# Second block of a two-block transformer: three groups of transposes two side steps later, and the compressed chain on VectorE in two pieces

## The chip, the cores and the metric

The kernel runs on one core of one Trainium2 chip. The metric is the device time of one execution in microseconds (us). Engines are named as in the profile: PE (TensorE), DVE (VectorE), ACT (ScalarE), POOL (GpSimd), SP (SyncE).

## What is computed

Two transformer blocks of two layers each, on 512 tokens of width 1024, in float32. The change is in the second block. One layer of it, cut to what matters:

```python
h = rmsnorm(x, norm_mix)
q_a, k_a, v_a, f_a, q_b, kv_b, g_b, gate_a, gate_b = split(h @ w_in)
o_a = fox_attention(...)                      # 8 heads with forget gates
y_a = from_heads(o_a) @ w_o_fox
q_n = partial_rope(to_heads(q_b, 8), pos)     # the turned queries
kc, vc, ks, vs, kw, vw = to_heads(kv_b)       # 2 key/value heads each
kc = partial_rope(compress_blocks(kc), ends)  # blocks of 32 tokens, stride 16
vc = compress_blocks(vc)                      # gelu(flat @ w1 + b1) @ w2 + b2
o_c = softmax(q_n kc) vc                      # 31 compressed blocks
o_s, o_w = selected and window branches       # over ks, vs and kw, vw
o_n = g0 * o_c + g1 * o_s + g2 * o_w
mixed = sigmoid(gate_a) * y_a + sigmoid(gate_b) * (o_n @ w_o_nsa)
x = x + mixed @ w_out
h = rmsnorm(x, norm_mlp); x = x + relu(h @ w_up)**2 @ w_down
```

With 512 tokens the selected and the window branch both see all causal keys, so both are plain causal attention.

## The kernel before, in words

Weights stream from HBM in units of up to 512 KB. SP loads a unit into RAW, ACT copies it to its upper float32r part Wh (L1466), DVE subtracts to get the lower part Wl (L2192), and PE makes three products per tile from the upper and lower parts (`three`, L641 to L643). The copies and subtractions run two units ahead of PE (`AHEAD`).

Each of PE, ACT and DVE has a program of its own, written out in order. Beside the main stream of linear layers each program keeps a list of side generators (`Sides`); `tick()` advances every open one to its next `yield`. The main stream calls `tick()` at the same places in the three programs, so one `yield` is one side step on all of them, and `idle(n)` lets n steps pass. The text numbers the steps T0, T1, ... from the first tick of the first `hidden` unit. In most units there are six products of 512 columns between two ticks; in the units of `hidden` (the compressor's first layer) three products of 256 columns. The stream from T0 is: four `hidden` units of keys, alternating with two `ga` units, then an `oa` unit, the same for values, then `ga`, `oa`, `ga`, `oa` and 32 steps of `gb` (T80 to T111), four ticks in each unit. Then `drain(ont)` ends the sides, and the `ob` products with ONh and ONl follow. Order within an engine is fixed: a waiting instruction holds all behind it.

The sides that matter, with PE's lines:

- `nsa_side` (L1246 ff.): after `idle(5)` six transposes of turned queries and keys (`heads_side`, L975 through `turn_rows`), `idle(5)`, then `mixing` over 64 items. An item is a query tile of 128 rows, a branch and a head. In step i, item i has its scores (L964, L965, mask L960), item i - 3 its exponentials transposed (L901), and a finished pair of items is multiplied with the values (L922, L923). Between scores and transposes lie the maximum on DVE (L2500), the exponential on ACT (L1663), the reciprocal on DVE (L2505, emitted one step after the maximum, behind the next item's maximum) and the normalising on POOL (L3291). Items come as tiles 3, 3, 0, 0 (4, 4, 1, 1 blocks of 128 keys) in the first 32 and 2, 2, 1, 1 in the last 32.
- `keys_side` (L1285 ff.): transposes of the compressor's inner layer HT (L1290), its second layer (L1299, L1300) and for keys a further transpose (L1307); once for keys (`kv` 0), begun after the first four `hidden` units, and once for values.
- `compressed_side` (L1314 ff.): for the later and then the earlier half of the tokens, scores on compressed keys (L1324, L1325), a pause, the transposes of their normalised exponentials CB (L1337); on DVE mask, maximum and shift (L3096 to L3102), sum, reciprocal, gates (L3106 to L3113), the multiplication (L3119); on ACT the exponential (L2056). At its end it adds `("compressed", l)` to `done`. `mixing` may not close a sum of the last 32 items before that (`need`).
- `on_side` splits the finished sums ONS into ONh (ACT) and ONl (DVE) once `mixing` and `compressed_side` are done.

Of the kernel before, what the change touches and what calls it, by code (L numbers as in the profile page):

```python
# [476 lines left out]
def idle(n):  # L477

    for _ in range(n):
        yield  # L480
# [22 lines left out]
def over(ap, n, where):  # L503
    v = ap.unsqueeze(where)
    shape = list(v.shape)
    shape[where] = n
    return v.to_broadcast(shape)
# [109 lines left out]
def tensor_program(pe, M, G, K, plan):  # L617
# [577 lines left out]
    for l in range(DEPTH):  # L1195
# [50 lines left out]
        def nsa_side():  # L1246
# [5 lines left out]
            while ("keys", l) not in done:  # L1252
                yield
            yield from idle(5)
            for j in range(6):
# [29 lines left out]
        def keys_side(kv):  # L1285
            yield from idle(2)
            b = fresh(f"ht{l} {kv}")
# [27 lines left out]
        def compressed_side():  # L1315
            for c in (1, 0):
# [12 lines left out]
                K.close(f"cs{l} {c}")  # L1329
                yield  # L1330
                yield
                yield
                yield
                b = fresh(f"ct{l} {c}")
# [111 lines left out]
def scalar_program(sc, M, G, K, plan, a):  # L1446
# [462 lines left out]
    for l in range(DEPTH):  # L1909
# [100 lines left out]
        def nsa_side():  # L2010
            while fox in sides.open:
                yield
            yield from blocks_side()
            done.add(("blocks", l))
            while ("keys", l) not in done:
                yield
            yield from idle(5)
            for j in range(6):
                yield from heads_side(j)
            yield from idle(5)  # L2020
            yield from mixing(nsa_bundles(l), take=nsa_take, need=("compressed", l), tail=5)
# [14 lines left out]
        def keys_side(kv):  # L2036
            yield from idle(3)
            name = f"ht{l} {kv}"
# [12 lines left out]
        def compressed_side():  # L2051
            for c in (1, 0):
# [3 lines left out]
                sc.activation(M.CB[:, :], M.CB[:, :], ACT.Exp).then_inc(G.c_exp, 1)  # L2056
                yield
                yield
                yield
                if c == 1:  # L2060
# [111 lines left out]
def vector_program(ve, M, G, K, plan):  # L2172
# [699 lines left out]
    for l in range(DEPTH):  # L2872
# [147 lines left out]
        def nsa_side():  # L3020
# [12 lines left out]
            for j in range(2):  # L3033
# [9 lines left out]
                yield  # L3043
            yield from idle(2)
            for j in range(6):
# [11 lines left out]
        def keys_side(kv):  # L3057
            yield from idle(7)
            name = f"w2{l} {kv}"
# [23 lines left out]
        def compressed_side():  # L3083
# [4 lines left out]
            for c in (1, 0):  # L3088
# [25 lines left out]
                if c == 0:  # L3114
                    p0 = p4[:, 0, :, :]
                    i = ve.tensor_tensor(p0, p0, over(M.CST[:, C_XV:C_XV + 32], 8, 1), ALU.mult)
                i.then_inc(*own.up())
                ve.wait_ge(*own.now())
                ve.tensor_tensor(p3, p3, over(f2.rearrange("p a b -> p (a b)"), 32, 2), ALU.mult).then_inc(G.c_p, 1)  # L3119
                yield  # L3120
                yield
# [240 lines left out]
```

## Time and profile before

| | us |
|---|---|
| median of 3 runs | 2856.04 |
| lowest and highest run | 2851.41, 2857.71 |
| the profiled execution | 2851.48 |
| its span in the trace | 2849.7 |
| PE busy, share of the span | 2730.9, 96% |
| DVE busy | 1556.9, 55% |
| ACT busy | 1157.8, 41% |
| POOL busy | 132.1, 5% |

The span is what the trace covers; 1.8 us lie around it. Matmuls are pipelined, so the busy time of PE counts overlaps as busy; where PE really stands still is seen in the time line, which puts the idle time before an instruction and its releaser in brackets. The changed part of each of the second block's two layers lies at about 1362 to 1588 and 2189 to 2415 us.

### The profile page before, as it was taken

The numbers are of one execution on the slowest core, as the hardware profiler recorded it, in microseconds if no ns is written. First come the engines' busy times: TensorE is split into PE (matmuls) and PEld (weight loads), VectorE is DVE, ScalarE is ACT, GpSimd is POOL, SyncE is SP. The second block draws the span as 40 slices with busy tenths as digits, with TensorE's granted clock in tenths as the row PEclk, the third lists the DMA queues.
The fourth block names the chain that finished last, engine by engine and source line by source line (L and its number), as shares of the span: only waits on it lengthen the run. The fifth ranks groups of instructions, "written<-read, shape, count | busy, mean of one in ns | idle before, by whom it ended". The sixth has DMA issues, their size and how long they took to land.

```text
span 2849.7 us, 34790 instructions
## 1 busy us (share of the span) xinstructions
PE 2730.9 (96%) x13497; PEld 2249.6 (79%) x13497; DVE 1556.9 (55%) x2788; ACT 1157.8 (41%) x2078; POOL 132.1 (5%) x221
## 2 busy tenths in 40 slices
PE   7899999999999999989899999999989899999997
PEld 6778888887788888767778888888768778888886
DVE  7856444467564444576766653343667665643343
ACT  3554222235542222355654433242465644342331
POOL 1000000000000000011122000000010211000000
PEclk9999999998999999999999999999999999999999
DMA  4102232321022323321311233333212211323332
GB/s 121 52 23 86 96 97 98 99 87 56 22 87 96 96 96 97 92 67 54 103 45 45 90 95 96 97 98 99 88 45 89 68 45 60 104 90 98 99 99 75
DMA packets 186358, 231.40 MB, mean 81 GB/s; under 512 B 11874, under 2 KB 140356, under 8 KB 186196
## 3 DMA queue, kind: packets, MB, share of 16 engines
q1 hardware_dynamic: 184500, 225.95, 25.4%
q0 software_dynamic: 976, 1.32, 0.3%
q8 instruction: 108, 1.77, 0.3%
q10 hardware_dynamic: 720, 1.92, 0.2%
q14 instruction: 54, 0.44, 0.1%
HBM read 227.05 MB, written 2.11 MB: 80 GB/s over the span
## 4 chain that ended last, share of the span: by engine, by line
PE 79%; DVE 12%; ACT 5%; issue 3%; DMA 0%; POOL 0%; ACTq 0%; DVEq 0%
PE bank L641 23%; PE bank L643 23%; PE bank L642 23%; DVE Wl L2192 2%; ACT Wh L1466 1%; PE bank L901 1%; PE bank L846 1%; DVE STT L2500 1%; PE bank L922 1%; PE bank L923 1%; PE bank L964 1%; PE bank L831 1%; PE bank L1155 1%; PE bank L965 1%; DVE KAl L2240 1%
## 5 line engine op out<-in xcount | busy, mean ns | idle before, releaser
L2192 DVE TENSOR_TENSOR Wl<-RAW,Wh 128x1024 fp32r<-128x1024 f32 (+3 forms) x434 | 510.5, 1199 | 367.1 <-ACT Wh L1466 366.2
L1466 ACT ACTIVATE Wh<-RAW 128x1024 fp32r<-128x1024 f32 (+3 forms) x434 | 437.7, 1032 | 402.7 <-PE bank L643 402.2
L641 PE MATMUL bank<-Hh,Wh 128*128 128x512 f32 (+1 forms) x1104 | 450.4, 408 | 6.3 <-DVE Wl L2192 4.9
L643 PE MATMUL bank<-Hh,Wl 128*128 128x512 f32 (+1 forms) x1104 | 433.3, 393 | 0.0
L642 PE MATMUL bank<-Hl,Wh 128*128 128x512 f32 (+1 forms) x1104 | 433.1, 392 | 0.0
L641 PE MATMUL bank<-HA,Wh 128*128 128x512 f32 x704 | 274.2, 390 | 0.0
L642 PE MATMUL bank<-HA,Wh 128*128 128x512 f32 x704 | 273.9, 389 | 0.0
L643 PE MATMUL bank<-HA,Wl 128*128 128x512 f32 x704 | 273.9, 389 | 0.0
L641 PEld LDWEIGHTS bank<-Hh,Wh 128*128 128x128 f32 (+1 forms) x1104 | 208.1, 188 | 48.9 <-DVE Wl L2192 6.2
L643 PEld LDWEIGHTS bank<-Hh,Wl 128*128 128x128 f32 (+1 forms) x1104 | 207.2, 188 | 46.9
L642 PEld LDWEIGHTS bank<-Hl,Wh 128*128 128x128 f32 (+1 forms) x1104 | 208.2, 189 | 36.3
L641 PE MATMUL bank<-A,Wh 128*128 128x512 f32 x608 | 236.5, 389 | 0.0
L642 PE MATMUL bank<-A,Wh 128*128 128x512 f32 x608 | 236.5, 389 | 0.0
L643 PE MATMUL bank<-A,Wl 128*128 128x512 f32 x608 | 236.5, 389 | 0.0
L1663 ACT ACTIVATE P<-bank,STT 128x384 f32<-128x384 f32 (+1 forms) x192 | 101.3, 528 | 137.8 <-DVE STT L2500 136.7
L643 PEld LDWEIGHTS bank<-HA,Wl 128*128 128x128 f32 x704 | 132.1, 188 | 27.6
L642 PEld LDWEIGHTS bank<-HA,Wh 128*128 128x128 f32 x704 | 132.1, 188 | 27.4
L641 PE MATMUL bank<-Wh,Hh 128*128 128x512 f32 (+2 forms) x384 | 149.2, 389 | 4.7 <-DVE Wl L2192 4.7
L641 PEld LDWEIGHTS bank<-HA,Wh 128*128 128x128 f32 x704 | 132.2, 188 | 27.1
L643 PE MATMUL bank<-Wh,Hl 128*128 128x512 f32 (+2 forms) x384 | 144.1, 375 | 0.0
L642 PE MATMUL bank<-Wl,Hh 128*128 128x512 f32 (+2 forms) x384 | 144.0, 375 | 0.0
L2324 DVE TENSOR_TENSOR XT<-bank,XT 128x512 f32<-128x512 f32 x112 | 77.1, 690 | 121.0 <-PE bank L643 120.8
(394 smaller groups left out, 4690.2 us busy)
## 6 DMA issues: line engine op xcount, KB each, us to landing
RAW<-in_w_up_dram SPq DMA_DIRECT2D x108, 512.0 KB, 3.6
RAW<-in_w_down_dram SPq DMA_DIRECT2D x108, 512.0 KB, 3.7
RAW<-in_w_in_dram SPq DMA_DIRECT2D x90, 512.0 KB, 3.5
RAW<-in_w_gate_dram SPq DMA_DIRECT2D x44, 512.0 KB, 3.6
RAW<-in_w_out_dram SPq DMA_DIRECT2D x28, 512.0 KB, 3.7
RAW<-in_cmp_w_dram SPq DMA_DIRECT2D x16, 512.0 KB, 3.8
RAW<-in_w_o_fox_dram SPq DMA_DIRECT2D x8, 512.0 KB, 3.4
RAW<-in_w_o_nsa_dram SPq DMA_DIRECT2D x8, 512.0 KB, 3.4
```

Source lines behind the costliest of these rows:

```text
L641: pe.matmul(o, sh, mh, start=first, stop=False)
L642: pe.matmul(o, sh, ml, start=False, stop=False)
L643: return pe.matmul(o, sl, mh, start=False, stop=last)
L831: x = pe.transpose(b[:, k * P:(k + 1) * P], M.PB[:, i % 4, k * P:(k + 1) * P], ident)
L846: x = pe.matmul(b[:, h * 64:(h + 1) * 64], M.PT[:, i % 3, k * P:(k + 1) * P], values(g, h, kb[k]), start=k == 0, stop=k == len(kb) - 1)
L901: x = pe.transpose(b[:, k * P:(k + 1) * P], e[:, k * P:(k + 1) * P], ident)
L922: pe.matmul(b[:, c:c + w], v, ph, start=B.opens(n) and k == 0, stop=False, skip_group_check=True)
L923: x = pe.matmul(b[0:64, c:c + w], v[:, 0:64], pl, start=False, stop=k == len(kb) - 1, skip_group_check=True)
L1466: sc.activation(M.Wh[:, v % NHL, 0:n], M.RAW[:, v % NRAW, 0:n], ACT.Copy).then_inc(G.w_hi, 1)
L1663: sc.activation(e, M.bank[K.of(name)][:, 0:e.shape[1]], ACT.Exp, bias=M.STT[:, 0, t, h:h + 1], accum_out=M.STT[:, 1, t, h:h + 1]).then_inc ...
L2192: ve.tensor_tensor(M.Wl[:, v % NRAW, 0:n], M.RAW[:, v % NRAW, 0:n], M.Wh[:, v % NHL, 0:n].bitcast(F32), ALU.subtract).then_inc(G.w_lo, 1)
L2324: ve.tensor_tensor(M.XT[:, k, :], M.bank[K.of(name)][:, :], M.XT[:, k, :], ALU.add).then_inc(*K.empties(name))
```

## The change

Nothing is computed otherwise; side steps are moved. Two more steps pass on all three engines before the transposes of turned queries and keys (with them all of `mixing`), before the transposes of HT, and between the compressed scores and the transposes of CB. On DVE the multiplication that ends the compressed chain (L3119) gets a step of its own, one after the sum, the reciprocal and the gates.

```diff
 # PE and ACT, nsa_side
-            yield from idle(5)
+            yield from idle(7)
             for j in range(6):
                 yield from heads_side(j)
 # PE, keys_side (ACT: 3 to 5, DVE: 7 to 9)
-            yield from idle(2)
+            yield from idle(4)
             b = fresh(f"ht{l} {kv}")
 # PE, compressed_side
                 K.close(f"cs{l} {c}")
-                yield
-                yield
-                yield
-                yield
+                yield from idle(6)
                 b = fresh(f"ct{l} {c}")
 # ACT, compressed_side
                 sc.activation(M.CB[:, :], M.CB[:, :], ACT.Exp).then_inc(G.c_exp, 1)
-                yield
-                yield
-                yield
+                yield from idle(5)
 # DVE, nsa_side
-            yield from idle(2)
+            yield from idle(4)
             for j in range(6):
                 yield from heads_side(j)
 # DVE, compressed_side
                 i.then_inc(*own.up())
+                yield
                 ve.wait_ge(*own.now())
                 ve.tensor_tensor(p3, p3, over(f2.rearrange("p a b -> p (a b)"), 32, 2), ALU.mult).then_inc(G.c_p, 1)
+                yield
                 yield
                 yield
```

By step numbers, PE has the first query transposes at T7 instead of T5, the first HT at T32 instead of T30, item i of `mixing` at T34 + i instead of T32 + i, the first transposes of CB at T75 instead of T71 and the second at T85 instead of T79. The compressed part is complete at T88 instead of T82. Item 45, the first of the last 32 to close a sum, is due at T82 before and at T84 now, so `mixing` is held one step before and five now, and ends at T107 instead of T101. The order of loads on SP and of the normalising on POOL is the same.

DVE, the compressed chain of the later half, before (CB are the compressed exponentials, CF the gates over their sums, STT the running maxima and sums of `mixing`):

```order
L2500 TENSOR_REDUCE STT_69<-bank 128x1 [waits bank5_full]
L2505 RECIPROCAL STT_69<-STT_69 128x1 [waits bank2_drained]
L2240 TENSOR_TENSOR PT_59<-bank,PT_58 128x2x128 [waits part_hi_made]
L3106 TENSOR_REDUCE RS_70<-CB_154 128x16 [waits cmp_exp_made]
L3110 RECIPROCAL CF_152<-RS_70 128x16 [waits vector_own]
L3113 TENSOR_TENSOR CF_152<-CF_152,GS_151 128x16 [waits bank1_drained,vector_own]
L3119 TENSOR_TENSOR CB_154<-CB_154,CF_152 128x512 [waits vector_own]
L2500 TENSOR_REDUCE STT_69<-bank 128x1 [waits bank7_full]
```

The same place in the changed kernel:

```order
L2500 RECIPROCAL STT_69<-STT_69 128x1 [waits bank6_drained]
L2235 TENSOR_TENSOR PT_59<-bank,PT_58 128x2x128 [waits part_hi_made]
L3101 TENSOR_REDUCE RS_70<-CB_154 128x16 [waits cmp_exp_made]
L3105 RECIPROCAL CF_152<-RS_70 128x16 [waits vector_own]
L3108 TENSOR_TENSOR CF_152<-CF_152,GS_151 128x16 [waits bank1_drained,vector_own]
L2357 TENSOR_TENSOR M_88_136<-bank,RBB_163 128x512 [waits bank1_drained,bank1_full]
L2495 TENSOR_REDUCE STT_69<-bank 128x1 [waits bank3_full]
L2500 RECIPROCAL STT_69<-STT_69 128x1 [waits bank2_drained]
L2235 TENSOR_TENSOR PT_59<-bank,PT_58 128x3x128 [waits part_hi_made]
L3115 TENSOR_TENSOR CB_154<-CB_154,CF_152 128x512 [waits vector_own]
L2495 TENSOR_REDUCE STT_69<-bank 128x1 [waits bank0_full]
```

A gate's evacuation (M) and one item's maximum, reciprocal and split now stand between the gates and the multiplication.

PE at T38, the third of the four short steps of the first `hidden` unit of values, before (XHL are the compressor's inputs, P the exponentials, KSh and KSl the keys, QN the queries):

```order
L641 MATMUL bank<-Wh_54,XHL_129 64x256
L642 MATMUL bank<-Wl_53,XHL_129 64x256
L643 MATMUL bank<-Wh_54,XHL_130 64x256
L901 MATMUL bank<-CST_61,P_9_57 128x128 [waits score_exp_normed,bank3_drained]
L964 MATMUL bank<-KSh_133,QN_132 128x128 [waits bank4_drained]
L965 MATMUL bank<-KSl_134,QN_132 128x128
L960 MATMUL bank<-CMB_65,IDB_64 128x128
L922 MATMUL bank<-PT_58,VN_125 128x256 [waits bank4_drained,bank7_drained,bank2_drained]
```

The same step in the changed kernel:

```order
L641 MATMUL bank<-Wh_54,XHL_129 64x256
L642 MATMUL bank<-Wl_53,XHL_129 64x256
L643 MATMUL bank<-Wh_54,XHL_130 64x256
L901 MATMUL bank<-CST_61,P_9_57 128x128 [waits score_exp_normed,bank2_drained]
L901 MATMUL bank<-CST_61,P_9_57 128x128 x3
L964 MATMUL bank<-KSh_133,QN_132 128x512 [waits bank3_drained]
L965 MATMUL bank<-KSl_134,QN_132 128x512
L960 MATMUL bank<-CMB_65,IDB_64 128x128
```

Before, this step transposes item 3 (one block) and makes the scores of item 6; now it transposes item 1 (four blocks) and makes the scores of item 4.

ACT where `mixing` is held for the compressed part, before (ONS are the sums, M the gates, PT the transposed exponentials):

```order
L1663 ACTIVATE P_9_57,STT_69<-bank,STT_69 128x256 [waits bank0_full,score_max_made]
L1984 ACTIVATE ONS_135<-bank 64x2x128 [waits bank3_full,bank6_full]
L1984 ACTIVATE ONS_135<-bank 64x2x128
L1466 ACTIVATE Wh_54<-RAW_52 128x1024 [waits bank3_full,raw_in1]
L1512 ACTIVATE PT_58<-bank 128x3x128 [waits bank3_full,bank6_full]
L1663 ACTIVATE P_9_57,STT_69<-bank,STT_69 128x256 [waits bank5_full,score_max_made]
L2098 ACTIVATE M_89_137<-M_89_137 128x512 [waits bank1_drained]
```

And in the changed kernel:

```order
L1660 ACTIVATE P_9_57,STT_69<-bank,STT_69 128x384 [waits bank0_full,score_max_made]
L1463 ACTIVATE Wh_54<-RAW_52 128x1024 [waits bank0_full,raw_in1]
L2093 ACTIVATE M_89_137<-M_89_137 128x512 [waits bank3_drained]
L2093 ACTIVATE M_89_137<-M_89_137 128x512 [waits bank6_drained]
L1463 ACTIVATE Wh_54<-RAW_52 128x1024 [waits weights_used,raw_in2]
L1509 ACTIVATE PT_58<-bank 128x2x128 [waits bank3_full,values_mixed]
L1660 ACTIVATE P_9_57,STT_69<-bank,STT_69 128x256 [waits bank7_full,score_max_made]
L1981 ACTIVATE ONS_135<-bank 64x2x128 [waits bank3_full,bank5_full]
```

A whole weight unit and both of its gates now pass without an exponential of `mixing` between them.

## Rows read from the trace of the kernel before

**Rows 1.** The page, part 4: the chain that ended last, by engine

```profile
PE 79%; DVE 12%; ACT 5%; issue 3%; DMA 0%; POOL 0%; ACTq 0%; DVEq 0%
```

**Rows 2.** Time line of PE, first pass: start us, us, instruction [idle before <-releaser]

```profile
1362.85 0.66 PE L975 MATMUL bank<-CST,QNS 128*128 128x128 f32 x4 [1.35 <-DVE QNS L2389]
...
1385.96 0.30 PE L1290 MATMUL bank<-CST,HT 64*128 64x64 f32 x2 [1.30 <-ACT HT L2033]
...
1389.38 0.47 PE L964 MATMUL bank<-KSh,QN 128*128 128x512 f32 x1 [1.11 <-issue]
...
1401.37 0.30 PE L901 MATMUL bank<-CST,P 128*128 128x128 f32 x1 [1.95 <-POOL P L3291]
...
1419.21 0.30 PE L901 MATMUL bank<-CST,P 128*128 128x128 f32 x1 [1.99 <-POOL P L3291]
...
1437.60 0.30 PE L901 MATMUL bank<-CST,P 128*128 128x128 f32 x1 [1.63 <-POOL P L3291]
...
1441.13 0.63 PE L901 MATMUL bank<-CST,P 128*128 128x128 f32 x4 [1.65 <-POOL P L3291]
...
1486.10 0.52 PE L901 MATMUL bank<-CST,P 128*128 128x128 f32 x3 [0.37 <-POOL P L3291]
...
1489.04 1.09 PE L1337 MATMUL bank<-CST,CB 128*128 128x128 f32 x4 [2.11 <-DVE CB L3119]
...
1515.45 0.63 PE L1337 MATMUL bank<-CST,CB 128*128 128x128 f32 x4 [1.66 <-DVE CB L3119]
```

**Rows 3.** Waits of PE, 2185 to 2410 (second pass): us in total, times, longest

```profile
PE bank L1337 <- DVE CB L3119: 3.8, 2, 2.1
```

**Rows 4.** Time line of PE, first pass: first products of a short and of long steps

```profile
1357.23 0.28 PE L641 MATMUL bank<-Wh,XHL 128*64 128x256 f32 x1
...
1358.59 0.40 PE L641 MATMUL bank<-Hh,Wh 128*128 128x512 f32 x1
...
1361.11 0.39 PE L643 MATMUL bank<-Hh,Wl 128*128 128x512 f32 x1
```

**Rows 5.** Time line of DVE, 1387 to 1403

```profile
1387.88 1.40 DVE L2552 TENSOR_TENSOR KSl<-bank,KSh 64x512 fp32r<-64x512 f32 x2
...
1398.80 1.21 DVE L2192 TENSOR_TENSOR Wl<-RAW,Wh 128x1024 fp32r<-128x1024 f32 x1
1399.93 0.67 DVE L2500 TENSOR_REDUCE STT<-bank 128x1 f32<-128x512 f32 x1
...
1402.05 0.27 DVE L2500 TENSOR_REDUCE STT<-bank 128x1 f32<-128x128 f32 x1
```

**Rows 6.** Time line of ACT, 1387 to 1403

```profile
1397.09 0.37 ACT L1663 ACTIVATE P<-bank,STT 128x128 f32<-128x128 f32 x1
...
1397.45 1.05 ACT L1466 ACTIVATE Wh<-RAW 128x1024 fp32r<-128x1024 f32 x1
...
1400.64 0.69 ACT L1663 ACTIVATE P<-bank,STT 128x512 f32<-128x512 f32 x1 [1.66 <-DVE STT L2500]
```

**Rows 7.** Time line of POOL, 1387 to 1403

```profile
1400.78 0.45 POOL L3291 TENSOR_SCALAR P<-P,STT,GS 128x128 f32<-128x128 f32 x1 [3.10 <-DVE STT L2505]
1402.03 0.78 POOL L3291 TENSOR_SCALAR P<-P,STT,GS 128x512 f32<-128x512 f32 x1 [0.81 <-DVE STT L2505]
```

**Rows 8.** Windows: us, busy time of each engine, granted share of PE's clock, DMA

```profile
1420.26:1423.67 3.41, 3.41 (x17) 3.31 (x16) 1.09 (x5) 1.68 (x8) 1.33 (x3) 0.50 0.25 68
1488.50:1491.94 3.44, 2.90 (x9) 2.55 (x10) 2.39 (x5) 1.51 (x3) 0.56 (x1) 0.50 0.05 16
2318.00:2321.40 3.40, 3.40 (x12) 2.72 (x11) 1.49 (x2) 1.28 (x3) 0.47 (x1) 0.50 0.00 0
```

**Rows 9.** Time line of PE, 1573 to 1589

```profile
1574.05 0.28 PE L923 MATMUL bank<-PT,VN 128*64 128x256 f32 x1
...
1587.81 0.39 PE L641 MATMUL bank<-ONh,Wh 128*128 128x512 f32 x1
```

**Rows 10.** Time line of DVE, 1573 to 1589

```profile
1579.29 1.29 DVE L2240 TENSOR_TENSOR ONl<-ONS,ONh 128x512 fp32r<-128x512 f32 x2 [1.22 <-ACT ONh L2090]
```

More of the change, by code:

```diff
@@ L2016, in nsa_side @@
                 yield
-            yield from idle(5)
+            yield from idle(7)
             for j in range(6):
@@ L2036, in keys_side @@
         def keys_side(kv):
-            yield from idle(3)
+            yield from idle(5)
             name = f"ht{l} {kv}"
@@ L2056, in compressed_side @@
                 sc.activation(M.CB[:, :], M.CB[:, :], ACT.Exp).then_inc(G.c_exp, 1)
-                yield
-                yield
-                yield
+                yield from idle(5)
                 if c == 1:
@@ L3057, in keys_side @@
         def keys_side(kv):
-            yield from idle(7)
+            yield from idle(9)
             name = f"w2{l} {kv}"
```

## The prediction

> **What bounds the kernel now.** I read four views in this order. The chain of waits says which engine sets the end: PE holds 79% of it, DVE and ACT the rest in small pieces [rows 1], so a wait counts only where PE itself stands idle. The time line of PE in the first pass of the changed part (layer 0 of the second block, about 1362 to 1588 us) then names each of its idle pieces in brackets [rows 2]: turned queries not ready (1.35 us), the compressor's inner layer HT not ready (1.30), the first score of the selected branch waiting without a named releaser (1.11), waits for POOL's normalised exponentials (1.95, 1.99, 1.63, 1.65, and a fifth of 0.37), and the two transposes of the compressed exponentials CB (2.11, 1.66). The waits of the second pass repeat this: the two CB waits there also add up to 3.8 [rows 3], so I work out one pass and double it. Third, what one side step covers: between two steps stand either three products of 256 columns or six of 512. Twelve of the first kind take 1358.59 - 1357.23 = 1.36 us, 0.34 a step; of the second kind eleven starts take 1361.11 - 1358.59 = 2.52 us, 0.229 each, 1.37 a step [rows 4]. Last, the granted clock by stretch [rows 8].
>
> **The change part by part.** No instruction is added or removed; all of them move, on PE, ACT and DVE alike, and with them POOL's normalising, which follows the items. The weight loads' queue issues in the same order as before. Number the steps T0, T1, ... from the first `hidden` unit. PE has short steps of 0.34 us at T0 to 3, 8 to 11, 16 to 19, 24 to 31, 36 to 39, 44 to 47, 52 to 55, long ones of 1.37 elsewhere up to T111.
>
> - *Turned queries, T5 to T7.* Two long steps, 2.7 us of products, now stand ahead, against a wait of 1.35 [rows 2]: gain 1.35.
> - *Inner layer's transpose, T30 to T32.* The hidden products it needs end at T27 as before, but the K transposes move as well, and ACT's copies of them stand ahead of the copy to HT. Between the last K transpose and this one, a short step becomes a long one: cover grows by 1.37 - 0.34 = 1.03, so of 1.30 some 0.3 stay. PE, no longer held before, then comes early to a weight unit whose Wl stands in DVE's queue behind the moved query and key parts; between nothing and the 1.30 itself I put 0.5. Gain 0.5 (ends 0 and 1.3).
> - *First score, T32 to T34.* It waits for the last key part KSl, whose DVE pair ends at 1387.88 + 1.40 = 1389.28 [rows 5], 0.1 ahead of it. From the last K transpose to the first score two short steps become long: cover +2.06, of which the shrunk waits ahead take 1.0. Of 1.11 about 0.2 stay. Gain 0.9 (ends 0 and 1.11).
> - *Compressed chain.* The transposes of CB come six steps after the last compressed score instead of four; the multiplication by the gates gets a step of its own, still with two PE steps behind it where there was one. The multiplication gains one long step with its item's products, over 1.37; what stood right ahead of it on DVE (sum, reciprocal, gates) gains two, over 2.74, against 2.11 and 1.66 [rows 2]. Both waits go: gain 3.77 (low end 2 x 1.37 = 2.74, if the multiplication alone was late).
>
> Gains: 1.35 + 0.5 + 0.9 + 3.77 = 6.52 us a pass.
>
> What is late next? The mixing starts two steps later, so the short steps now meet other items. Items come in fours: two of 4 blocks, two of 1 (for the first half). At T36, T44 and T52 a unit begins, and the next Wh and Wl are made there. Before, the item ahead of that border had one block: its exponential (0.37) is followed on ACT by Wh (1.05), then on DVE by Wl (1.21), the next item's maximum (0.67) and only then its reciprocal, and POOL (0.45) [rows 5 to 7]. That is the wait of 1.95. Now it is a 4-block item: exponential 0.69 and POOL 0.78 instead of 0.37 and 0.45, +0.65; the maximum in between is of one block, 0.27 for 0.67 [rows 5], -0.40; and PE's own work in the three steps is some 0.15 less. So the wait stays at the same step and grows by 0.4, three times: loss 1.2. The first item now has its turn inside the short steps too: loss 0.4, a fifth of a border wait. In the last stretch a second item waited already (1.65 [rows 2]); with two large items at once I add 0.4. Ends for all of this: a gain of 1.65 (that second wait goes) and a loss of 5 (a second wait of 1.65 in each stretch).
>
> Around T73 the score chain loses cover: the shift by the maximum, two DVE passes over CB, now stands a step ahead of a border, so that exponential, Wh, Wl and reciprocal follow it in one line. The wait at this place is 0.37 now, at 1486.10 [rows 2]. I let it grow by 0.7, between 0 and the 1.6 that would make it a border wait of 1.99.
>
> Last, the tail. The compressed part is complete at T88 instead of T82, and the mixing may not close its second half before that: it is held five steps instead of one. So it ends six steps later, four steps ahead of the products with ONh instead of ten. From the last value product (1574.05 + 0.28) to those products there are 13.5 us now [rows 9], and there will be 4 x 1.37 = 5.5. The last ONl is ready 1580.58 - 1574.33 = 6.25 us after it [rows 9, 10], and is asked for by the fourth group of three products, 3 x 0.69 = 2.1 after the start, at 7.5. It fits by about 1.3; I put 0.4 (ends 0 and 3.8, below).
>
> Losses: 1.2 + 0.4 + 0.4 + 0.7 + 0.4 = 3.1. Net gain 6.52 - 3.1 = 3.4 a pass, **6.8 us** in both.
>
> **The clock.** Behind the wait of 1.99 and behind that of 2.11 PE ran at 0.50 of full speed, 1.2 GHz, for 3.41 us each; the stretch from 2318.00 in the second pass is one more [rows 8]. Each costs about half its length, 1.7. Two of the three stand behind CB waits that go: a credit of 3.4. But three border waits a pass grow beyond 2 us, and one of those of 1.99 drew such a stretch already; I let one more a pass do so: 0 in sum, ends -3.4 and +3.4. The Trainium skill (TensorE: Matmul & The Clock Gate, section "Why this matters for your kernels") lets the speed fall only behind idle gaps longer than any in these rows; by it the clock would give and take nothing, and the sum would be the waits alone, 6.8 again. The rows differ from it: the granted 0.50 stands right behind 1.99 and 2.11.
>
> The profiled execution took 2851.48 us; the sum makes 2844.7 of it. It is the low end of the three runs (2851.41 to 2857.71); from their median, 2856.04, the same 6.8 gives **2849.2**, which I predict. A measurement of this kernel can tell about 0.2%, 5.7 us, from no change.
>
> **The rivals.**
> - *The short steps take all of it back.* If both large items wait in each of the three stretches, as the pair of 1.63 and 1.65 does, the loss there is about 5 instead of 2: net 6.52 - 6.1 = 0.4 a pass, 2855. For it: that pair; against: the first two stretches show one wait each.
> - *Slower: the tail.* If the evacuations of the last gates stand ahead of the taking of the last sums on ACT and DVE, two on each engine (0.7 apiece, as 512-column pieces take [rows 5, 6]) and one Wh and Wl (1.05, 1.21), 5.0 us in all, the chain is 11.3 against 7.5: PE waits 3.8 and a half-speed stretch behind it costs 1.7. That is 5.5 instead of 0.4: net 6.52 - 8.2 = 1.7 slower a pass, 2859. It decides once the tail costs PE more than 0.4 + 3.4 = 3.8 a pass. Against it: the same chain took 6.25 with evacuations around it.
> - *Clean.* The border waits stay as they are, the tail costs nothing and the clock's credit comes in full: (6.52 - 0.7) x 2 + 3.4 = 15, 2841. For it: the smaller maximum that now stands in the border chain; against: the larger exponential there.
>
> **How the numbers follow.** The forecast (net 3 to 10 us faster) gets 0.62, of which about two thirds are beyond 5.7 us; the first rival 0.19; the slower one 0.09, most of it beyond the bound once a noisy median is added; the clean one 0.10. So faster 0.41 + 0.10 = 0.51, the same 0.21 + 0.19 + 0.01 = 0.41, slower 0.08. The range runs from the clean case, 2841, to between the first rival and the slower one, 2857, and leaves out about 2 in 10.
>
> **What would show it.** In the changed profile: no PE wait for QNS and none for CB; HT and first score under 0.5; one POOL wait of about 2.3 at each of the three borders, at a product with four transposes instead of one; a new POOL wait near 1 us between the two transposes of CB; 24 products between the last value product and the first with ONh, with under 0.5 of waiting there. Wrong: a CB wait over 0.5; border waits in pairs; over 2 us of waiting at the first products with ONh; a half-speed stretch behind more than two of a pass's three borders.

## The result, and the profile after

The changed kernel takes 2840.26 us (median of four runs, 2838.24 to 2840.70) against 2855.0 for the kernel before (four runs): a ratio of 0.9948, 95% interval 0.9936 to 0.996, or 14.7 us faster (11 to 18). The forecast was 6.8 us. The direction was right, the size less than half; the time lies 0.7 us below the range and at the rival "clean".

| us | before | after |
|---|---|---|
| median | 2855.0 | 2840.26 |
| profiled execution | 2851.48 | 2838.24 |
| its span | 2849.7 | 2836.4 |
| PE busy | 2730.9 | 2727.1 |
| DVE busy | 1556.9 | 1555.4 |
| POOL busy | 132.1 | 132.4 |

The chain of waits of the changed kernel has three points less of PE than [rows 1]; DVE and ACT still come in small pieces. So again a wait counts where PE stands.

```profile
PE 76%; DVE 14%; ACT 5%; issue 4%; DMA 0%; POOL 0%; ACTq 0%; DVEq 0%
```

The time line of PE shows where. First the kernel before: a value product of the first attention in either layer, whose wait of 1.43 the change does not touch (the mark of the pass), the first product with ONh in the second pass (that of the first pass is in [rows 9]), and, at 1467.94, a wait for PT in the first pass that [rows 2] leave out.

```profile
1295.04 0.38 PE L922 MATMUL bank<-PT,VF 128*128 128x256 f32 x1 [1.43 <-DVE PT L2240]
...
1467.94 0.44 PE L964 MATMUL bank<-KSh,QN 128*128 128x384 f32 x1 [0.69 <-DVE PT L2240]
...
2121.79 0.38 PE L922 MATMUL bank<-PT,VF 128*128 128x256 f32 x1 [1.43 <-DVE PT L2240]
...
2416.56 0.39 PE L641 MATMUL bank<-ONh,Wh 128*128 128x512 f32 x1
```

The same marks after, and between the first two of them every wait of PE in the changed part of the first pass (start, length, the instruction; idle time before it and its releaser in brackets; behind the edits, line numbers are three to five lower than before, so L3288 here is L3291 there):

```profile
1295.22 0.38 PE L922 MATMUL bank<-PT,VF 128*128 128x256 f32 x1 [1.43 <-DVE PT L2235]
...
1383.99 0.50 PE L641 MATMUL bank<-Hh,Wh 128*128 128x512 f32 x1 [0.43 <-DVE Wl L2187]
...
1389.56 0.47 PE L964 MATMUL bank<-KSh,QN 128*128 128x512 f32 x1 [0.53 <-issue]
...
1395.01 0.63 PE L901 MATMUL bank<-CST,P 128*128 128x128 f32 x4 [0.96 <-POOL P L3288]
...
1397.54 1.09 PE L901 MATMUL bank<-CST,P 128*128 128x128 f32 x4 [1.31 <-POOL P L3288]
...
1416.19 0.63 PE L901 MATMUL bank<-CST,P 128*128 128x128 f32 x4 [2.07 <-POOL P L3288]
...
1434.85 0.63 PE L901 MATMUL bank<-CST,P 128*128 128x128 f32 x4 [1.95 <-POOL P L3288]
...
1437.02 0.30 PE L901 MATMUL bank<-CST,P 128*128 128x128 f32 x1 [0.36 <-POOL P L3288]
...
1439.92 0.38 PE L922 MATMUL bank<-PT,VN 128*128 128x256 f32 x1 [0.27 <-DVE ONS L2994]
...
1445.16 0.63 PE L901 MATMUL bank<-CST,P 128*128 128x128 f32 x4 [0.52 <-POOL P L3288]
...
1489.31 0.52 PE L901 MATMUL bank<-CST,P 128*128 128x128 f32 x3 [1.10 <-POOL P L3288]
...
1493.80 0.47 PE L641 MATMUL bank<-OAh,Wh 128*128 128x512 f32 x1 [0.36 <-DVE PT L2235]
...
1581.94 0.39 PE L641 MATMUL bank<-ONh,Wh 128*128 128x512 f32 x1
...
1583.67 0.50 PE L641 MATMUL bank<-ONh,Wh 128*128 128x512 f32 x1 [0.20 <-DVE ONl L2235]
...
2116.90 0.38 PE L922 MATMUL bank<-PT,VF 128*128 128x256 f32 x1 [1.43 <-DVE PT L2235]
...
2402.30 0.39 PE L641 MATMUL bank<-ONh,Wh 128*128 128x512 f32 x1
```

By the marks the 13.3 us by which the span is shorter split exactly. Up to the first mark 0.18 is lost. The first pass, mark to ONh, shrinks from 1587.81 - 1295.04 = 292.77 to 286.72: 6.05 gained. From there to the second mark 0.98 is lost (533.98 to 534.96). The second pass shrinks from 294.77 to 285.40: 9.37. From its ONh to the end 0.96 is lost (433.14 to 434.10). 6.05 + 9.37 - 0.18 - 0.98 - 0.96 = 13.30.

Neither QNS nor CB has a wait any more; the brackets of the changed part of the first pass, 15.1 in [rows 2] and 0.69 for PT, 15.8 together, are down to 10.1. The two passes differ by the clock. Windows of the kernel before (us, busy time of each engine, granted share of PE's clock, DMA), beside the stretches of [rows 8]:

```profile
1395.00:1430.00 35.00, 31.06 (x192) 25.45 (x191) 22.60 (x62) 20.12 (x53) 9.46 (x16) 0.95 0.20 61
1484.00:1496.00 12.00, 9.52 (x51) 7.64 (x50) 8.17 (x20) 5.63 (x15) 2.45 (x4) 0.86 0.15 44
2225.00:2240.00 15.00, 13.02 (x75) 10.70 (x74) 10.34 (x30) 8.67 (x25) 3.98 (x7) 0.89 0.18 58
2290.00:2325.00 35.00, 31.72 (x179) 25.93 (x177) 22.30 (x57) 15.80 (x41) 5.79 (x10) 0.90 0.16 46
2297.49:2300.90 3.41, 3.41 (x12) 2.73 (x11) 0.25 (x1) 0.47 (x3) 0.32 (x1) 0.50 0.00 0
```

and of the changed kernel, where in the changed part nothing but these two is below 1.00:

```profile
1390.00:1425.00 35.00, 30.65 (x184) 24.79 (x183) 22.93 (x59) 19.11 (x51) 8.79 (x14) 0.90 0.20 61
2210.00:2245.00 35.00, 30.11 (x185) 23.74 (x183) 24.14 (x61) 20.63 (x53) 8.32 (x14) 0.95 0.20 61
```

A share of 0.95 in 35 us is 1.7 us of the fast clock lost, one stretch of 3.4 us at 1.2 GHz. Before there are two stretches in the first pass and three in the second, 8.6 us lost; now two and one, 5.2. (The 35 us from 2290 hold two: that of [rows 8] and the one in the last window, behind a wait of 0.69 for PT, which [rows 8] leave out as they do the one after 2225.) So of the second pass's 9.37 about 6.0 are waits, as in the first pass, where the number of stretches stays, and 3.4 are clock.

### The profile page after: what moved, and what is told of

Its sections match the earlier page's. It is cut to its first block, busy times and chain, and to the rows that moved or that the text cites. A ratio compares the mean times of both kernels' runs of the same rounds, so it can differ in the third digit from the quotient of the medians.

```text
span 2836.4 us, 34790 instructions
## 1 busy us (share of the span) xinstructions
PE 2727.1 (96%) x13497; PEld 2244.0 (79%) x13497; DVE 1555.4 (55%) x2788; ACT 1157.3 (41%) x2078; POOL 132.4 (5%) x221
## 3 DMA queue, kind: packets, MB, share of 16 engines
HBM read 227.05 MB, written 2.11 MB: 81 GB/s over the span
## 4 chain that ended last, share of the span: by engine, by line
PE 76%; DVE 14%; ACT 5%; issue 4%; DMA 0%; POOL 0%; ACTq 0%; DVEq 0%
PE bank L641 22%; PE bank L642 22%; PE bank L643 22%; DVE Wl L2187 2%; ACT Wh L1463 2%; PE bank L901 1%; PE bank L846 1%; DVE STT L2495 1%; PE bank L922 1%; PE bank L964 1%; PE bank L1155 1%; PE bank L965 1%; PE bank L831 1%; PE bank L923 1%; DVE KAl L2235 1%
```

## The experiments

The kernels ran in three sets of four, each set beside runs of the kernel before (medians 2855.81, 2855.48 and 2856.19). Diffs are against the kernel before unless said otherwise and show PE's program; ACT and DVE get the same number of steps at their places.

**1. The compressed chain's part alone.**

```diff
                 K.close(f"cs{l} {c}")
-                yield
...
+                yield from idle(6)
```

(`...` stands for three more `yield`. On DVE the multiplication gets a step of its own, as in the change.)

> The compressed chain's part alone (six steps between its scores and its transposes, the multiplication in a step of its own); the mixing and the inner layer stay where they were. If the parts simply add up by the forecast's terms: both CB waits go (3.77 us a pass), 0.7 comes back around T73 and 0.4 at the tail: 5.3 us faster in both passes. If they add up by what the changed kernel's rows show (1.10 - 0.37 and 0.36 around T73, 0.96 at the tail): 1.95 a pass, 3.9 faster, and up to 3.4 more where the half-speed stretches behind the CB waits go with them. If the parts need each other (the mixing's moved items were part of the cure): a CB wait over 0.5 us stays, and the gain is under 2 us.

Measured: 2845.66 (seven runs), ratio 0.9968 (0.9957 to 0.9979), 10.2 us faster. The two CB waits in the first pass of its PE time line:

```profile
1497.32 0.66 PE L1334 MATMUL bank<-CST,CB 128*128 128x128 f32 x4 [0.69 <-DVE PT L2235]
...
1523.58 0.63 PE L1334 MATMUL bank<-CST,CB 128*128 128x128 f32 x4 [0.27 <-DVE CB L3115]
```

They fall from 2.11 and 1.66 to 0.69 (now put down to PT) and 0.27, the other waits stay: 2.8 us a pass. No stretch at 0.50 stands behind the first any more. The tail costs nothing: 433.16 from ONh to the end, as before. From mark to ONh its passes take 289.99 and 290.37, 7.2 us less than before in both, which fits 5.6 of waits and one half-speed stretch less. The medians say 10.2; what the rest is, this profile does not show. By the medians this part is two thirds of the gain.

**2. Turned queries and mixing two steps later, alone.**

```diff
-            yield from idle(5)
+            yield from idle(7)
             for j in range(6):
                 yield from heads_side(j)
```

> The turned queries and with them the mixing two steps later, nothing else. By the forecast's terms: QNS 1.35 and the first score 0.9 go, the borders cost 1.2 + 0.4 + 0.4: 0.25 a pass, 0.5 us faster in both. By the changed kernel's rows: QNS 1.35, first score 0.58 and the PT wait 0.69 go, the borders cost 0.22: 2.4 a pass, 4.8 faster. If the parts need each other: the copies of the moved K transposes now stand on ACT ahead of the copy to HT, whose transposes have not moved, so the HT wait grows from 1.30 towards 3, the CB waits do not shrink, and the kernel is 0 to 4 us slower.

Measured: 2857.19 (eleven runs), 1.0005 (0.9996 to 1.0014). QNS is gone, and two waits grow in its place:

```profile
1385.78 0.31 PE L1290 MATMUL bank<-CST,HT 64*128 64x64 f32 x2 [2.57 <-ACT HT L2033]
...
1488.25 1.09 PE L1337 MATMUL bank<-CST,CB 128*128 128x128 f32 x4 [3.98 <-DVE CB L3119]
```

HT waits 2.57 instead of 1.30, and the first CB 3.98 instead of 2.11. The third theory held. The forecast had seen the first of the two ("ACT's copies of them stand ahead of the copy to HT"), not the second: the moved items also make the compressed chain later.

**3. The inner layer's transposes two steps later, alone.**

```diff
         def keys_side(kv):
-            yield from idle(2)
+            yield from idle(4)
```

> The transposes of the inner layer HT two steps later, nothing else. By the forecast's terms: of HT's 1.30 some 0.3 to 0.5 stay and Wl may come late by as much: 1 to 2 us faster in both passes. By the changed kernel's rows (HT gone, Wl 0.43 new): 0.87 a pass, 1.7 faster. If the parts need each other: HT's wait goes, but the first score right behind it waits longer by the same amount (1.11 to about 2), since PE comes to it earlier: 0 to 1 us faster.

Measured: 2856.80 (eleven runs), 1.0005 (0.9996 to 1.0014). HT's wait of 1.30 goes and comes back at the next unit, as 1.64 for Wl:

```profile
1388.28 0.50 PE L641 MATMUL bank<-Hh,Wh 128*128 128x512 f32 x1 [1.64 <-DVE Wl L2192]
```

The second CB waits 2.35 for 1.66, while the waits for PT and POOL ahead of the first CB shrink by as much (0.69 to 0.32, 0.37 to none). None of the theories had Wl at 1.64; the gain is nil, as the third said.

**4. The whole change, with the multiplication in the step of the gates.**

```diff
                 i.then_inc(*own.up())
-                yield
                 ve.wait_ge(*own.now())
                 ve.tensor_tensor(p3, p3, over(...), ALU.mult).then_inc(G.c_p, 1)
+                yield
                 yield
```

(DVE, against the changed kernel.)

> The whole change but for the split: on DVE the multiplication follows the gates in the same step, as before, with two more steps behind it. If the split matters (the multiplication in the way of the next item's maximum, reciprocal and POOL): the POOL wait near T74, 1.10 in the changed kernel, grows by the multiplication's time and the kernel is 1 to 3 us slower than the changed one. If the later transposes alone do the work: the CB waits are gone as well, all PE waits within 0.3 us of the changed kernel's, the time within 2 us of it (about 0.995 of the kernel before).

Measured: 2842.04 (five runs), 0.9952 (0.9938 to 0.9966). The POOL wait is the changed kernel's 1.10, and no CB wait stands in either pass:

```profile
1494.91 0.52 PE L901 MATMUL bank<-CST,P 128*128 128x128 f32 x3 [1.09 <-POOL P L3288]
```

The split buys nothing that shows; the two later steps do the work.

**5. Mixing and inner layer later, the compressed chain as before.**

> Turned queries, mixing and inner layer two steps later, the compressed chain as before: the change without its third part. If the three parts simply add up (compressed chain alone 10 us faster, mixing alone 1 slower, inner layer alone 1 slower): about 2 us slower than the kernel before. If mixing and inner layer only help each other (HT wait 2.57 and Wl wait 1.64 of the two alone fall to the changed kernel's 0.43) and the compressed chain is a matter of its own: QNS, HT and PT waits go, CB waits stay at 2.1 and 1.7, 2 us a pass, about 4 us faster. If the moved mixing makes the compressed chain late as well (CB waits 4.0 and 1.5 as with the mixing alone): 1.7 of those 2 us are given back and it is 0 to 1 us faster.

The diffs of 2 and 3 together. Measured: 2852.91 (eleven runs), 0.9993 (0.9985 to 1.0002): 2.6 us faster, if anything. HT's wait is gone and Wl's is 0.43, so these two parts help each other. But:

```profile
1493.63 0.63 PE L1337 MATMUL bank<-CST,CB 128*128 128x128 f32 x4 [3.93 <-DVE CB L3119]
...
1521.04 0.63 PE L1337 MATMUL bank<-CST,CB 128*128 128x128 f32 x4 [2.66 <-DVE CB L3119]
```

6.6 us of CB waits a pass instead of 3.8. So the parts do not add up in waits: the compressed part alone takes 2.8 us a pass from the brackets, but 4.9 once the mixing is moved (15.0 here, 10.1 in the changed kernel). A step at this place is also worth more than its 1.37 us of products, as the items' own products lie in it: from the last compressed score of the later half PE has 11.65 us here until it stands still for CB (1478.05 to 1489.70), and 17.70 in the changed kernel until the transposes of CB (1475.11 to 1492.81), of which 1.10 is the new wait for POOL. So two steps hold 4.95 us of work, not 2.74.

**6. The kernel before, with PE kept at work in the CB waits.**

```diff
                 b = fresh(f"ct{l} {c}")
+                for k in range(16 if c else 12):
+                    pe.transpose(b[:, k % 4 * P:k % 4 * P + P], ident, ident)
                 pe.wait_ge(G.c_p, 2 * l + 2 - c)
```

> The kernel before, with PE kept at work in the two CB waits: 16 and 12 extra transposes of the identity into the bank that the real transposes then overwrite, some 1.4 and 1.1 us of the waits of 2.11 and 1.66. If PE's clock falls because PE stands idle there: the half-speed stretches behind the CB waits (at 1488 and 2316 in the kernel before) are gone, the waits' ends stay, and the kernel is 1.7 to 3.4 us faster by its clock alone. If these stretches have nothing to do with the idle time: they remain, and the time is that of the kernel before within 1 us.

The extra transposes are overwritten by the real ones. Measured: 2851.65 (eleven runs), 0.9989 (0.998 to 0.9997), 3.8 us faster by the medians. Of the wait before the first CB 0.28 is left. Windows from there on, and around the second pass's:

```profile
1488.00:1500.00 12.00, 11.37 (x79) 9.59 (x77) 9.09 (x23) 6.68 (x17) 3.01 (x5) 1.00 0.15 45
2290.00:2325.00 35.00, 33.57 (x206) 27.80 (x205) 23.24 (x58) 16.13 (x42) 5.76 (x10) 0.95 0.16 46
```

The first window is at 1.00 where the kernel before had 0.86, the second at 0.95 where it had 0.90: the two stretches behind the CB waits are gone, the third (behind the PT wait at 2296) is not. PE's real work did not start earlier. Behind the waits that were not filled, stretches come and go from one profile to the next: the first pass has two at its borders where the kernel before has one, and is no shorter (292.87 us from mark to ONh, 292.77 before); the second has none at its borders and takes 291.64 instead of 294.77. So the time is better taken from the medians, and their 3.8 us (1 to 6 by the interval) fit the 3.4 of two stretches. The clock's credit is real.

**7. Mixing five steps later, the compressed chain as in the change.**

```diff
-            yield from idle(5)
+            yield from idle(10)
             for j in range(6):
                 yield from heads_side(j)
```

(And the diff of 1.)

> Turned queries and mixing five steps later, the compressed chain as in the change, the inner layer where it was before. With five (as with one) step the two items that stand at a border of units are both of one block: exponential 0.37, maximum 0.28 and POOL 0.45 beside Wh and Wl, and the first border passes before there are exponentials to transpose. If the borders are set by the items' size there: the wait at the first border goes (2.3 in the changed kernel), the other two fall to about 1.5 each or less, the first score's and PT's waits go; HT's stays near 1.5; 3 to 5 us a pass better than the changed kernel, 2830 to 2834. If a border costs about 2 us whatever stands there (the four measured border waits were 1.95 to 2.07): the same time as the changed kernel, within 3 us, or slower by a tail that now ends three steps later (up to 4 us a pass).

Measured: 2816.99 (four runs), 0.9864 (0.9851 to 0.9877): 38.5 us faster than the kernel before, 23 better than the change. These are all its waits of the first pass from QNS on, but for one of 0.25:

```profile
1387.70 0.31 PE L1290 MATMUL bank<-CST,HT 64*128 64x64 f32 x2 [1.16 <-ACT HT L2030]
...
1400.66 0.63 PE L901 MATMUL bank<-CST,P 128*128 128x128 f32 x4 [1.16 <-POOL P L3288]
...
1412.56 0.30 PE L901 MATMUL bank<-CST,P 128*128 128x128 f32 x1 [0.71 <-POOL P L3288]
...
1428.21 0.30 PE L901 MATMUL bank<-CST,P 128*128 128x128 f32 x1 [0.23 <-POOL P L3288]
```

```profile
1360.00:1575.00 215.00, 211.26 (x1274) 174.95 (x1273) 150.11 (x343) 126.48 (x291) 38.93 (x64) 1.00 0.23 69
```

The border waits are 0.71 and 0.23, and in neither pass does the clock fall (this window is the first pass's, from QNS on). The passes last 275.53 and 275.18 from mark to ONh. It is more than either theory gave: the borders were put at 1.5 and have 0.71 and 0.23, the last stretch, T73 and the tail have no wait left, and the changed kernel's three stretches at 1.2 GHz are gone.

**8. Mixing five steps later and nothing else.**

> As the run before, but with the compressed chain as in the kernel before: turned queries and mixing five steps later and nothing else. If the CB waits come from the mixing's work ahead of the chain on DVE, ACT and POOL at this place: they change with the items there, to under 1 us each, and the kernel is within 5 us of the run before. If the compressed chain is late by its own length: CB waits of 2.1 and 1.7 or more stay, and it is 7 to 10 us slower than the run before.

Measured: 2820.28 (four runs), 0.9877 (0.9862 to 0.9892). One number is changed, 5 to 10 on PE and ACT and 2 to 7 on DVE. The second CB waits no longer, the first half as long as before:

```profile
1496.32 0.63 PE L1337 MATMUL bank<-CST,CB 128*128 128x128 f32 x4 [1.05 <-DVE CB L3119]
```

So the CB waits depend mostly on which items stand beside the chain (3.98 for the first with two steps in run 2, 1.05 with five), not on its length alone; a wait just over the 1 us of the first theory is left.

**9 and 10. Mixing one step later, and four steps later.** The compressed chain is as in the change; the first `idle` is 6, then 9.

> Turned queries and mixing one step later instead of two, the compressed chain as in the change, the inner layer as before. The items at a border are then both of one block, as with five steps, but the first border is met. If the border waits are set by which items stand there: waits of about 0.7 at the first two borders and 0.2 at the third (as with five steps: 0.71 and 0.23), the first score's wait stays partly, and the time is 2820 to 2826, 14 us or more under the changed kernel though the mixing starts earlier. If it was only the later start that helped with five steps: the borders keep about 2 us each and the time lies between those of the compressed part alone (2846) and of the change (2840).

> Turned queries and mixing four steps later, the rest as in the run before: the same items at the borders as in the kernel before (one block, then four), but the first border is passed before there are exponentials to transpose. If the border waits are set by which items stand there: 1.99 at the second border, 1.63 and 1.65 at the third as in the kernel before, the first gone: 4.3 us a pass slower than with five steps, 2825 to 2832 with the clock. If the later start is what matters: within 3 us of the run with five steps, 2815 to 2820.

Measured: 2826.59 (0.9899, 0.9884 to 0.9914) with one step, 2837.31 (0.9938, 0.9922 to 0.9955) with four, four runs each. The waits at the first two borders with one step:

```profile
1399.74 0.30 PE L901 MATMUL bank<-CST,P 128*128 128x128 f32 x1 [1.05 <-POOL P L3288]
...
1416.26 0.30 PE L901 MATMUL bank<-CST,P 128*128 128x128 f32 x1 [0.72 <-POOL P L3288]
```

and with four:

```profile
1397.40 1.09 PE L901 MATMUL bank<-CST,P 128*128 128x128 f32 x4 [2.94 <-POOL P L3288]
...
1415.92 0.30 PE L901 MATMUL bank<-CST,P 128*128 128x128 f32 x1 [1.98 <-POOL P L3288]
```

Later is not better: with one step 1.05, 0.72 and 1.21, with four 2.94, 1.98 and 1.42. With four the second border has the kernel before's 1.99 again, as its items are the same ones. Both expectations missed at one end, and the time with four steps lies above both of its ranges: with one step the third border does not fall to 0.2 (1.21, and another 0.59 follows there; why, stays open) and HT waits 2.27; with four the first border is not passed, since the first transposes come in the last step of its short stretch. The kernels with none, one, two, four and five steps agree with this: what decides is which items of the group of four stand at a border. With one step and with five they are the two small ones, with large ones ahead whose products PE works off meanwhile (this last is argued, not tested by itself).

**11. Five steps later, with the inner layer's two steps as in the change.**

> As the run with five steps, but with the inner layer two steps later as in the change. If the wait for HT (1.16 with five steps) simply goes: 2.3 us faster, about 2815. If it only moves on to what comes behind it (as with the inner layer alone, where HT's wait became one for Wl of 1.64): the same time or slower, 2817 to 2825, with new waits at the second layer or at the compressed chain.

The diffs of 7 and 3. Measured: 2830.39 (four runs), 0.9912 (0.9897 to 0.9926): 13 us slower than without this part, more than any theory gave. HT's 1.16 is gone and comes back several times over: there is 0.60 ahead of the second layer's products (L1299), POOL's 1.16 and 0.71 are 1.84 and 1.06, there is one of 1.09 for PT between the two CBs, and at the first CB

```profile
1485.50 0.63 PE L1334 MATMUL bank<-CST,CB 128*128 128x128 f32 x4 [1.19 <-DVE CB L3115]
```

and the tail's wait for ONl, 0.20, which run 7 did not have. Each pass also has a stretch at 1.2 GHz again (from 1400.14 and from 2308.08). Here the part of the change that it needs at two steps does harm.

**12. The changed kernel, with PE kept at work in the border waits.**

```diff
             b = fresh(f"{tag} t{i}")
+            if need:
+                for k in range({1: 8, 9: 16, 17: 16}.get(i, 0)):
+                    pe.transpose(b[:, k % 4 * P:k % 4 * P + P], ident, ident)
             pe.wait_ge(*norm.due())
```

> The changed kernel, with PE kept at work in the border waits: 8, 16 and 16 extra transposes of the identity into the bank that the real ones then overwrite, some 0.7, 1.4 and 1.4 us of waits of 1.3, 2.1 and 1.95. If PE's clock falls because it stands idle at the borders: the half-speed stretches there (at 1396 and 1416 in the first pass, 2220 in the second of the changed kernel) are gone, and the time is 3 to 5 us under the changed kernel's, 2835 to 2837. If not: stretches as before, 2840.

Measured: 2837.14 (four runs), 0.9936 (0.9921 to 0.9951). Around the borders, where the changed kernel had 0.90 and 0.95:

```profile
1390.00:1430.00 40.00, 37.81 (x241) 30.77 (x241) 28.89 (x70) 25.14 (x61) 9.69 (x16) 1.00 0.22 64
2210.00:2245.00 35.00, 32.84 (x216) 26.78 (x216) 25.33 (x64) 21.92 (x55) 8.79 (x14) 1.00 0.22 63
```

The passes last 283.80 and 283.83 from mark to ONh, 2.9 and 1.6 less than the changed kernel's, for two and one stretches. The medians, 3.1 apart, agree, but the intervals of the two ratios overlap, so the time alone does not show it. The windows do: nothing in either pass is below 1.00, while run 4, with the same border waits not filled, has 0.90 and 0.95 around them as the changed kernel has, and run 5 has 0.95 and 0.95.

## Why the prediction was wrong

Term by term, us of a pass, from the brackets of [rows 2] and of the time line above:

| term | forecast | measured |
|---|---|---|
| QNS | +1.35 | +1.35 |
| HT, less the new wait for Wl | +0.5 | 1.30 - 0.43 = +0.87 |
| first score | +0.9 | 1.11 - 0.53 = +0.58 |
| CB | +3.77 | +3.77 |
| PT wait at 1467.94 | not counted | +0.69 |
| three borders, first item, last stretch | -2.0 | -0.22 |
| around T73 | -0.7 | 0.37 - 1.10 - 0.36 = -1.09 |
| tail | -0.4 | -0.97 |
| net | +3.4 | 6.05 - 0.97 = +5.1 |

The measured terms above the tail sum to 5.95, and the marks give 6.05. The PT wait is one of PE's idle pieces that [rows 2] leave out, so the prediction could not count it. Both passes: 10.2 instead of 6.8. The clock: 3.4 instead of 0. Together 13.5, and the profiled executions are 13.3 apart.

**The step that failed** is the one on the short steps: "the wait stays at the same step and grows by 0.4, three times", with 0.4 more for the first item and 0.4 for the last stretch. Forecast as a loss of 2.0 us a pass, it cost 0.22, which is 3.6 us of the gain in both passes. Measured, the first border went from 1.95 to 0.96 + 1.31 = 2.27, the second from 1.99 to 2.07, the last stretch from 1.63 + 1.65 = 3.28 to 1.95 + 0.36 + 0.27 + 0.52 = 3.10. The mechanism is there in the main: the long wait of each border now stands at a product with four transposes. (At the first border it is a pair, 0.96 and 1.31, which the prediction had named as a sign of being wrong; together they make the 2.3 that it forecast for one.) At the second border the chain from the exponential (with Wh behind it on ACT) over Wl, the maximum and POOL to the transposes reads, before:

```profile
1415.19 0.36 ACT L1663 ACTIVATE P<-bank,STT 128x128 f32<-128x128 f32 x1
...
1416.62 1.23 DVE L2192 TENSOR_TENSOR Wl<-RAW,Wh 128x1024 fp32r<-128x1024 f32 x1 [0.61 <-ACT Wh L1466]
...
1417.77 0.68 DVE L2500 TENSOR_REDUCE STT<-bank 128x1 f32<-128x512 f32 x1
...
1418.62 0.45 POOL L3291 TENSOR_SCALAR P<-P,STT,GS 128x128 f32<-128x128 f32 x1 [3.58 <-DVE STT L2505]
```

and after:

```profile
1411.93 0.69 ACT L1660 ACTIVATE P<-bank,STT 128x512 f32<-128x512 f32 x1
...
1413.68 1.23 DVE L2187 TENSOR_TENSOR Wl<-RAW,Wh 128x1024 fp32r<-128x1024 f32 x1 [1.32 <-ACT Wh L1463]
...
1414.82 0.28 DVE L2495 TENSOR_REDUCE STT<-bank 128x1 f32<-128x128 f32 x1
...
1415.28 0.77 POOL L3288 TENSOR_SCALAR P<-P,STT,GS 128x512 f32<-128x512 f32 x1 [2.54 <-DVE STT L2500]
```

From the exponential to the transposes it was 1419.21 - 1415.19 = 4.02 and is 1416.19 - 1411.93 = 4.26: 0.24 longer, just as 0.65 - 0.40 says. But the prediction added 0.15 for less work of PE in the three steps, which no row gives: PE's own work is the same (3.36 and 3.33 us from the item's mask product to the wait). And it left out that the exponential starts 0.19 sooner behind that product (1.14 for 1.33 us), as the copy of PT ahead of it on ACT is of one block: 0.24 + 0.03 - 0.19 = 0.08, as measured at this border. The 0.4 for the first item and the 0.4 for the last stretch came from no row either; the last stretch even got 0.18 shorter.

**The clock** was the second step: "I let one more a pass do so: 0 in sum". The two stretches behind the CB waits went, as forecast; in run 6 they are gone with these waits filled. At the borders one stretch was added in both passes together, not two: before there is one in each pass (from 1420.26, and in the window from 2225), after it two and one. And the stretch from 2297.49, behind the PT wait, went too, which the prediction had not counted. Three gone and one new make the 3.4, half of the shortfall. How many fall at the borders differs between profiles of the same waits (runs 4 and 5), so this size is that of one pair of profiles. By the Trainium skill (TensorE: Matmul & The Clock Gate, section "Why this matters for your kernels") no gap in the changed part of either kernel would lower the clock, all being shorter than the ones that it names; runs 6 and 12 show that here they did, and what it costs.

**What held.** No wait for QNS and none for CB; the new POOL wait of 1.10 near T73 (forecast near 1; it stands ahead of the first transposes of CB, not between the two); HT and first score, together 1.45 gained against 1.4, each within its ends. That the other misses add up to almost nothing is luck: 0.37 more at HT, 0.69 at PT, and 0.32 less at the first score, 0.39 around T73, 0.57 at the tail.

**What was off the other way.** The tail: PE has 1581.94 - 1576.63 = 5.3 us there, forecast 5.5, and the last sums were to fit by 1.3. They do not, because of something near what the slower rival named: an evacuation of the last gates, here ahead of the splitting of the last sums. ACT in the changed kernel:

```profile
1581.74 0.63 ACT L2093 ACTIVATE M<-M 128x512 f32<-128x512 f32 x1 [2.18 <-DVE M L2357]
```

The copy to the second pair of ONh (1582.27) stands behind this sigmoid M, which waited 2.18 for DVE; so the second ONl comes late. The bracket has only 0.20, but start to start PE loses 0.36 there and 0.12 at the next product, and almost as much again (0.32 and 0.11) among the products with MXh, where Wl comes 0.15 late. Runs 1, 7 and 8 have 8.0 us there instead of 5.3 and lose nothing.

**The rivals.** "Clean" had the time right and its parts wrong: it let the tail cost nothing and T73 0.7 (1.09 and 0.97 came), and had no gain at PT. "The short steps take all of it back" failed, as no border of the first pass took back more than 0.32.

**The base.** The sum was made against a profiled execution of 2851.48 with five stretches in the changed part, and the difference then taken from the median, which is right only if the clock outside the changed part averages out; here it nearly did (13.3 in the profiles, 14.7 in the medians).

## What to carry to other kernels

Count a wait's growth along its chain from rows, and leave out what no row gives: losses put in above that hid a quarter of the real gain here (3.6 of 14.7). Where a program interleaves a stream with items of alternating size, try the phase before the distance: moving one `idle` from 5 to 10 was worth more than the three parts of this change, moving it to 9, even with the compressed part, half of that. And test parts in pairs: two of these parts alone were worth nothing or less, because each pushed its wait to the neighbour that the other part moves.

## What was not expected of the hardware

The length of a single wait does not say whether PE's clock falls behind it. In the first pass of the changed kernel the granted share is 0.50 from the transposes at 1397.54 on (four of them take 1.09 us instead of 0.63), behind waits of 0.96 and 1.31 that lie 2.5 us apart; in the second pass, behind 2.09 and behind 1.95, it stays at 1.00. What runs 6 and 12 show is that it did not fall behind the waits in which PE was given work, even if nobody needs the result: the granted share stayed at 1.00 there with 28 extra transposes a pass (run 6) and with 40 (run 12). The Trainium skill (TensorE: Matmul & The Clock Gate, section "Part 4: PE-mode transpose") says that transposes do not count as the engine's being busy in the same way; the trace differs from it as far as holding the clock goes. Whether transposes alone would raise it, no run here shows.

Executions also differ where the change does not reach: the first mark, ahead of everything that was moved, lies at 1295.04 us in the profile of the kernel before and at 1301.02 in that of run 4, with a granted share of 0.99 up to there in the one and 0.98 in the other. That is as much as the 0.2% that a measurement of this kernel can tell.
